# Dense S5 matrices of a two-layer trunk as 64x64 tiles in four quadrants, with the S5 input fetched in two halves

## What is computed

```python
def _s5_mixer(u, a_re, a_im, b_re, b_im, c_re, c_im, d_skip, log_dt, w_glu):
    ug = u.reshape(B, L, S5_GROUPS, S5_GROUP)           # 64 groups of 16 channels
    dt = jnp.exp(log_dt)[:, None]
    mag = jnp.exp(a_re * dt)                            # a_re, a_im: (64, 64)
    ab_re, ab_im = mag * jnp.cos(a_im * dt), mag * jnp.sin(a_im * dt)
    ...
    bb_re = cf_re * b_re - cf_im * b_im                 # (64, 64, 16)
    bb_im = cf_re * b_im + cf_im * b_re
    bu_re = jnp.einsum('blgi,gni->blgn', ug, bb_re)
    bu_im = jnp.einsum('blgi,gni->blgn', ug, bb_im)
    _, _, x_re, x_im = lax.associative_scan(...)        # x_t = ab * x_(t-1) + bu_t
    y = jnp.einsum('blgn,gin->blgi', x_re, c_re) - jnp.einsum('blgn,gin->blgi', x_im, c_im)
    y = jax.nn.gelu(y.reshape(B, L, S5_WIDTH) + d_skip * u)
    return y * jax.nn.sigmoid(y @ w_glu)
```

## Time and profile before

| | us |
|---|---|
| median of 3 runs | 1902.22 |
| lowest and highest | 1891.05, 1905.71 |
| the profiled execution | 1898.04 |
| its span (first to last instruction) | 1896.2 |
| TensorE busy in it | 1762.7 |
| VectorE, ScalarE, GpSimd busy | 961.6, 693.6, 794.6 |
| mean granted clock of TensorE | 0.963 |

### The profile page before, as it was taken

How to read it: one execution, slowest core, us unless ns; L and a number is a source line. 1 busy time by engine, 2 the same in 40 slices (tenths; PEclk the granted TensorE clock), 3 DMA queues, 4 the chain that set the end, 5 groups by cost and what they waited for, 6 DMA issues and landing times.

```text
span 1896.2 us, 28935 instructions
## 1 busy us (share of the span) xinstructions
PE 1762.7 (93%) x11959; PEld 1572.6 (83%) x11959; DVE 961.6 (51%) x1527; ACT 693.6 (37%) x1236; POOL 794.6 (42%) x492
## 2 busy tenths in 40 slices
PE   6977898999998999999997999989999799999997
PEld 5876798999887999999996987777788688888886
DVE  8997124423428985277653222533243688734223
ACT  3453332444543213233333543344456222224222
POOL 2644565433224324433343686653332332344442
PEclk8898899999999999999998999999999999999999
DMA  9455236222364573436552433542223656433432
GB/s 148 135 167 149 82 88 142 74 79 69 89 152 148 190 200 99 104 90 174 172 156 61 125 90 90 118 123 70 76 79 102 180 191 184 141 100 91 144 104 85
DMA packets 360137, 230.38 MB, mean 121 GB/s; under 512 B 49604, under 2 KB 346744, under 8 KB 357448
## 3 DMA queue, kind: packets, MB, share of 16 engines
q1 hardware_dynamic: 349480, 198.40, 39.8%
q10 hardware_dynamic: 10528, 30.15, 4.7%
HBM read 180.82 MB, written 47.15 MB: 120 GB/s over the span
## 4 chain that ended last, share of the span: by engine, by line
PE 66%; DVE 10%; DMA 7%; POOL 6%; ACT 4%; SPq 3%; issue 3%; ACTq 0%; DVEq 0%; POOLq 0%
PE ring L825 49%; DMA sb_w_raw<-in_w_in 5%; POOL sb_w_lo L667 3%; PE ring L784 3%; DVE sb_s_prod L1572 2%; DVE sb_s_mat_prod L1572 2%; PE aux L1177 2%; PE ring L806 1%; PE aux L1085 1%; SPq L570 1%; PE aux L1164 1%; PE aux L1130 1%; DVE sb_s_rot L2071 1%; PE aux L1106 1%; DVE sb_o_branch L1655 1%
## 5 line engine op out<-in xcount | busy, mean ns | idle before, releaser
L667 POOL TENSOR_TENSOR sb_w_lo<-sb_w_raw,sb_w_hi 128x1024 fp32r<-128x1024 f32 x246 | 608.7, 2476 | 1018.3 <-ACT sb_w_hi L1229 1016.2
L1229 ACT ACTIVATE sb_w_hi<-sb_w_raw 128x1024 fp32r<-128x1024 f32 x246 | 259.9, 1057 | 623.5 <-DMA sb_w_raw<-in_w_in 394.4
L825 PE MATMUL ring<-sb_u_hi,sb_w_hi 128*128 128x264 f32 (+1 forms) x2112 | 362.9, 325 | 31.5 <-DVE sb_tmp_dve L1642 21.4
L825 PEld LDWEIGHTS ring<-sb_u_hi,sb_w_hi 128*128 128x128 f32 x2112 | 308.6, 199 | 70.1 <-DVE sb_tmp_dve L1642 23.8
L825 PE MATMUL ring<-sb_u_lo,sb_w_hi 128*128 128x264 f32 (+1 forms) x2112 | 338.2, 311 | 0.0
L825 PE MATMUL ring<-sb_u_hi,sb_w_lo 128*128 128x264 f32 (+1 forms) x2112 | 334.5, 309 | 0.0
L825 PEld LDWEIGHTS ring<-sb_u_lo,sb_w_hi 128*128 128x128 f32 x2112 | 298.8, 191 | 21.2
L825 PEld LDWEIGHTS ring<-sb_u_hi,sb_w_lo 128*128 128x128 f32 x2112 | 294.2, 188 | 20.9
L1261 ACT ACTIVATE sb_tmp_act<-ring 128x528 f32<-128x528 f32 (+1 forms) x112 | 67.4, 602 | 133.0 <-PE ring L825 130.1
L825 PE MATMUL ring<-sb_y_hi,sb_w_hi 128*128 128x264 f32 (+1 forms) x504 | 88.1, 325 | 3.1 <-ACT sb_w_hi L1229 3.1
L1492 ACT ACTIVATE sb_att_scores<-sb_att_scores,sb_att_neg_max 128x208 f32<-128x208 f32 x128 | 58.4, 458 | 82.1 <-DVE sb_att_neg_max L1860 82.1
(11 more groups left out here) (328 smaller groups left out, 2585.4 us busy)
## 6 DMA issues: line engine op xcount, KB each, us to landing
sb_w_raw<-in_w_in SPq DMA_DIRECT2D x166, 512.0 KB, 4.1
sb_s_loaded<-s_matrices ACTq DMA_DIRECT2D x16, 1808.0 KB, 8.1
s_matrices<-sb_s_phase SPq DMA_DIRECT2D x16, 528.0 KB, 3.2
s_matrices<-sb_s_mbt SPq DMA_DIRECT2D x16, 512.0 KB
s_matrices<-sb_s_ca SPq DMA_DIRECT2D x16, 512.0 KB
sb_w_raw<-in_w_gla_out SPq DMA_DIRECT2D x16, 512.0 KB, 3.8
sb_w_raw<-in_w_attn_out SPq DMA_DIRECT2D x16, 512.0 KB, 3.8
sb_w_raw<-in_s_w_glu SPq DMA_DIRECT2D x16, 512.0 KB, 3.7
```

What stands on the lines that cost most here:

```text
L667: pool.tensor_tensor(WL[:, w], WR[:, w], WH[:, w].bitcast(F32), ALU.subtract).then_inc(lo_ready, 1)
L825: last = pe.matmul(RING[:, 2 * r + hf, 0:c1 - c0], w[:, n % SLOTS, kt, :], moving(b[0], xx[:, kt], c0, c1), start=(term == 0 and kt == 0), ...
L1229: act.activation(WH[:, w], WR[:, w], ACT.Copy).then_inc(hi_ready, 1)
```

## The change

The matrices `mbt`, `cam` and `toep` keep only their non-zero 64x64 parts: 64 columns for a quad in place of 128 (toep: 64 partitions' worth on the diagonal), 2336 floats per partition in place of 3616, some 1168 KB for a tile. Quads 1 and 3 have the states of their two groups in swapped halves, so that two quads together use all four quadrants. `step_inputs` has 16 logical matmuls of 64x64 in place of 8, `step_outputs` 24 in place of 12, in four groups (toep, cam, toep, cam) with three waits of TensorE for its own matmuls between them (`row_tiles_done`); the wait for the state stands behind the first toep group. Z4 is fetched in halves of four tiles, eight DMAs of 16 rows each, at ag0 and at ag3. The store to YD has 2 DMAs, the load of YZ 8 in place of 4, `load_mats` 3 in place of 1, `load_b` 8 in place of 2. `products` writes two full-partition outputs in place of four half ones. The transposes L881 become 16 matmuls of 64x64, the toep matmuls read a new buffer `mb0` with zeros in it, filled by four small copies of ScalarE at the head of `matrices_out`, for which TensorE waits (`first_power`). The skip uses a 16-column unit matrix. At the start the rows are also copied and transposed in swapped order. GpSimd zeroes `toep` and `mb0` in place of `cam`, `toep` and `mbm`.

```diff
@@ -77,7 +77,7 @@
 
-S5_FLOATS = 2 * QUADS * P + 2 * QUADS * P + QUADS * P + 2 * QUADS * STEPS
+S5_FLOATS = 2 * QUADS * 64 + 2 * QUADS * 64 + 2 * QUADS * STEPS + QUADS * 64
...
@@ -92,6 +92,7 @@
 S5_IN = 2
+Z4_PART_AT = {("ag", 0): 0, ("ag", 3): 1}
...
@@ -446,6 +451,16 @@
 
+        def load_b(queue, m):
+
+            for ri, src in enumerate((s5_b_re, s5_b_im)):
+                dst = MB[m]["b"][:, ri].rearrange("p (a x) i -> p a x i", x=2)
+                src = src[m].rearrange("(a x g) n i -> x g n a i", x=2, g=2)
+                for g in range(2):
+                    for x in range(2):
+                        rows = slice(S5_STATE * (g ^ x), S5_STATE * (g ^ x) + S5_STATE)
+                        queue.dma_start(dst[rows, :, x], src[x, g]).then_inc(s5_par, 16)
+
...
@@ -606,24 +616,33 @@
                         sp.wait_ge(z_spilled, 16 * KT * (ly + 1))
-                        for p in range(STRIDE):
-                            sp.dma_start(Z4[32 * p:32 * p + 32].rearrange("i j q c -> i (j q) c"),
-                                         ZD[ly, :, :, STRIDE - 1 - p, :].rearrange("j (q i) c -> i (j q) c", q=QUADS)
-                                         ).then_inc(steps_loaded, 16)
+                    if name in Z4_PART_AT:
+                        half = Z4_PART_AT[name]
+                        js = slice(4 * half, 4 * half + 4)
+                        for g in range(2):
+                            for p in range(STRIDE):
+                                r0 = 64 * g + 16 * p
+                                sp.dma_start(Z4[r0:r0 + 16, js].rearrange("i j q c -> i (j q) c"),
+                                             ZD[ly, js, :, STRIDE - 1 - p, :]
+                                             .rearrange("j (q g i) c -> g i (j q) c", q=QUADS, g=2)[g]
+                                             ).then_inc(steps_loaded[half], 16)
...
@@ -658,7 +677,7 @@
 
-            for name in ("cam", "toep", "mbm"):
+            for name in ("toep", "mb0"):
...
@@ -861,6 +880,9 @@
 
+            def half_rows(half):
+                return slice(64 * half, 64 * half + 64)
+
...
@@ -878,17 +900,22 @@
                     for q in range(QUADS):
-                        last = pe.transpose(AX_[:, 2 * h + ri, P * q:P * q + P],
-                                            MB[m]["mbm"][:, ri, q].rearrange("p a b -> p (a b)"), ID[:])
+                        for g in range(2):
+                            ins, outs = half_rows(g ^ (q % 2)), half_rows(g)
+                            c0 = 128 * ri + 64 * (q // 2)
+                            last = pe.matmul(AX_[outs, 2 * h + q % 2, c0:c0 + 64],
+                                             MB[m]["mbm"][ins, ri, q].rearrange("p a b -> p (a b)"), ID[ins, ins],
+                                             start=True, stop=True)
                 last.then_inc(aux_full[h], 1)
                 h = aux_take(m, ("toep", j))
-                cam, mbm = MB[m]["cam"][:, j % 2], MB[m]["mbm"]
+                cam, mb0 = MB[m]["cam"][:, j % 2], MB[m]["mb0"]
+                pe.wait_ge(first_power, 8 * m + j + 1)
                 for ri in range(2):
                     for q in range(QUADS):
-                        pe.matmul(AX_[32 * q:32 * q + 32, 2 * h, 0:P], mbm[:, ri, q, 0],
+                        pe.matmul(AX_[32 * q:32 * q + 32, 2 * h, 0:64], mb0[:, ri, q],
                                   cam[:, ri, q, 0:4].rearrange("p a b -> p (a b)"),
                                   start=(ri == 0), stop=False)
-                last = pe.matmul(AX_[:, 2 * h, 0:32], ID[:], MB[m]["dsk"][:], start=False, stop=True)
+                last = pe.matmul(AX_[:, 2 * h, 0:S5_GROUP], ID[:], MB[m]["dsk"][:], start=False, stop=True)
...
@@ -1154,30 +1184,46 @@
 
-                    if j == 0:
-                        pe.wait_ge(steps_loaded, 64 * ly + 64)
-                    pe.wait_ge(mats_in[j % 2], 16 * (4 * ly + j // 2) + 16)
+                    if j % 4 == 0:
+                        pe.wait_ge(steps_loaded[j // 4], 128 * ly + 128)
+                    pe.wait_ge(mats_in[j % 2], 48 * (4 * ly + j // 2) + 48)
                     mbt = mat_part(MSB[:, j % 2], "mbt").rearrange("p (r q m) -> p r q m", r=2, q=QUADS)
                     for ri, name in enumerate(("vre", "vim")):
                         h = aux_take(ly, (name, j))
-                        for q in range(QUADS):
-                            last = pe.matmul(AX_[:, 2 * h + q // 2, STEPS * (q % 2):STEPS * (q % 2) + STEPS],
-                                             mbt[:, ri, q, :], Z4[:, j, q, :], start=True, stop=True)
+                        for a in range(2):
+                            for x in range(2):
+                                for g in range(2):
+                                    ins, outs = half_rows(g), half_rows(g ^ x)
+                                    last = pe.matmul(AX_[outs, 2 * h + x, STEPS * a:STEPS * a + STEPS],
+                                                     mbt[ins, ri, 2 * a + x, :], Z4[ins, j, 2 * a + x, :],
+                                                     start=True, stop=True)
                         last.then_inc(aux_full[h], 1)
 
                 def step_outputs(j):
 
-                    pe.wait_ge(x_state, 8 * ly + j + 1)
                     cam = mat_part(MSB[:, j % 2], "cam").rearrange("p (r q m) -> p r q m", r=2, q=QUADS)
                     toep = mat_part(MSB[:, j % 2], "toep").rearrange("p (q m) -> p q m", q=QUADS)
                     h = aux_take(ly, ("y", j))
-                    for q in range(QUADS):
-                        dst = AX_[:, 2 * h + q // 2, STEPS * (q % 2):STEPS * (q % 2) + STEPS]
+                    for a in range(2):
+                        n = 3 * (8 * ly + j) + 2 * a + 1
+                        if a:
+                            last.then_inc(row_tiles_done, 1)
+                            pe.wait_ge(row_tiles_done, n - 1)
+                        for x in range(2):
+                            for g in range(2):
+                                rows, q = half_rows(g), 2 * a + x
+                                last = pe.matmul(AX_[rows, 2 * h + x, STEPS * a:STEPS * a + STEPS],
+                                                 toep[rows, q], Z4[rows, j, q, :], start=True, stop=False)
+                        last.then_inc(row_tiles_done, 1)
+                        pe.wait_ge(row_tiles_done, n)
+                        pe.wait_ge(x_state, 8 * ly + j + 1)
                         for ri in range(2):
-                            pe.matmul(dst, cam[:, ri, q],
-                                      XX[:, ri, q, :], start=(ri == 0), stop=False)
-                        last = pe.matmul(dst, toep[:, q], Z4[:, j, q, :],
-                                         start=False, stop=True)
+                            for x in range(2):
+                                for g in range(2):
+                                    ins, q = half_rows(g ^ x), 2 * a + x
+                                    last = pe.matmul(AX_[half_rows(g), 2 * h + x, STEPS * a:STEPS * a + STEPS],
+                                                     cam[ins, ri, q], XX[ins, ri, q, :],
+                                                     start=False, stop=(ri == 1))
...
@@ -1291,13 +1337,22 @@
 
+                act.wait_ge(mats_ready, 8 * m + j + 1)
+                for half in range(2):
+                    rows = slice(64 * half, 64 * half + 64)
+                    for x in range(2):
+                        c0 = S5_GROUP * (half ^ x)
+                        last = act.activation(MB[m]["mb0"][rows, :, x::2, c0:c0 + S5_GROUP],
+                                              MB[m]["mbm"][rows, :, x::2, 0], ACT.Copy)
+                last.then_inc(first_power, 1)
                 if j:
                     spilled(act, m, j - 1)
                 h = aux_result(act, m, ("mbt", j))
-                act.activation(MB[m]["mbt"][:].rearrange("p r q m -> p r (q m)"), aslot(h), ACT.Copy
+                act.activation(MB[m]["mbt"][:].rearrange("p r (a x) m -> p x (r a) m", x=2),
+                               aslot(h)[:, :, 0:256].rearrange("p x (b m) -> p x b m", b=4), ACT.Copy
                                ).then_inc(aux_free[h], 1)
                 h = aux_result(act, m, ("toep", j))
-                last = act.activation(MB[m]["toep"][:, 3 * 32:], AX_[:, 2 * h, 0:P], ACT.Copy)
+                last = act.activation(MB[m]["toep"][:, 48:], AX_[:, 2 * h, 0:64], ACT.Copy)
...
@@ -1329,7 +1386,11 @@
                 act.wait_ge(phase_spilled, 16 * 8 * (ly + 1))
-                act.dma_start(MSB[:, j % 2], MATD[ly, j]).then_inc(mats_in[j % 2], 16)
+                o = S5_FLOATS - QUADS * 64
+                act.dma_start(MSB[:, j % 2, 0:o], MATD[ly, j, :, 0:o]).then_inc(mats_in[j % 2], 16)
+                toep = mat_part(MATD[ly, j], "toep").rearrange("(t g i) x -> g t i x", t=STRIDE, g=2)
+                for g in range(2):
```

(39 more changed lines are left out.)

96 lines of the change are left out of this document (51 added, 45 removed).

## The result

| | before | after |
|---|---|---|
| median of 20 runs, us | 1902.98 | 1892.12 |
| lowest, highest | 1891.05, 1909.54 | 1884.84, 1900.03 |
| the profiled execution | 1898.04 | 1896.51 |
| its span; mean clock | 1896.2; 0.963 | 1894.7; 0.958 |

After to before is 0.994, 95% interval 0.9925 to 0.9956: 0.6% faster, 10.9 us. Forecast were 1872 us and a gain of some 30. The gain is about a third of the forecast, and "faster by over 1%" did not come. The time lies in the range of 1851 to 1897, but only because the range was drawn wide enough for rivals A in pairs and B (1889 and 1888); the forecast's own range ended at 1884.

What follows compares the result with a forecast made beforehand. TensorE, busy 93% of the span, was taken as the bound, with 133 us of waiting. Terms -19.6 - 5 - 5 - 10 + 11 + 1.7 = -26.9 gave 1872 us; own range 1851 to 1884, with rivals 1851 to 1897.

Steps and rivals of the forecast that it cites:

- A in pairs: S5 tiles: quadrants work only two at a time, +13 in place of -5, 1889 us; chance 0.09.
- B: S5 front: splitting the Z4 fetch moves nothing, SP's issue holds the weights; -3 for -19.6, 1888 us; chance 0.11.
- Step 1: Front of the S5 stage, both layers: halved fetch and smaller matrices land weights earlier; -19.6 us, ends -27 and -3.
- Step 2 and 3: S5 middle: later wait for the state, -5 us; steady tiles: 4.2 us against 4.57, -5 for 14 periods.
- Rival A: S5 tiles: not four quadrants at once; two at a time 1889 us, all in series 1952; chance 0.13.
- Step 4: Layer 0's matrices: VectorE saves 13 us, toep's waits for ScalarE copies mostly absorbed; net -10 us, ends -16 and +18.
- Step 5: Layer 1's matrices: VectorE's gain hidden, TensorE waits for ScalarE's copies; +11 us, ends +6 and +30.
- Rival C: Both matrix sets: waits for ScalarE replace those for VectorE, +18 and +30, 1918 us; chance 0.08.
- Step 6: Start: six S5P copies for two and two more transposes ahead of the first norm; +1.7 us, ends 0 and 3.

Runs made afterwards that it cites:

- Experiment 8: Kernel before, with Z4 fetched whole at ag0 by eight DMAs of 16 rows in place of four of 32: 1925.58 us, ratio 1.0116.
- experiment 9: Changed kernel with each half of Z4 fetched by two DMAs of 64 rows, the spill writing in read order by four DMAs a tile: 1888.92 us, ratio 0.9934.
- experiment 1: Changed kernel with ScalarE's first-power copies of layer 1's matrices moved ahead of the block's turn: 1867.21 us, ratio 0.9821 to the kernel before.
- experiment 2: Changed kernel with a tile's output matmuls reordered so that independent matmuls stand before each self-wait: 1885.26 us, ratio 0.9908.
- experiment 5: Changed kernel with both layer 1's first-power copies ahead of the block's turn and the reordered output matmuls: 1870.28 us, ratio 0.9816.
- experiment 7: Changed kernel with the first-power copies moved ahead in both layers' sets, in layer 0's ahead of log_sigmoid: 1865.33 us, ratio 0.9803.
- experiment 3: Changed kernel with all of Z4 fetched at ag0 by eight DMAs of 16 rows, not in halves: 1920.11 us, ratio 1.009.
- experiment 11: The kernel of experiment 9 with Z4 fetched whole at ag0, by two DMAs of 64 rows: 1910.83 us, ratio 1.0051.
- experiment 6: Changed kernel with the second half of Z4 fetched at mg2 1 in place of ag3: 1894.98 us, ratio 0.9955.

## Why the prediction was off, step by step

**Step 1, the front: -19.6 forecast, -11.8 measured.** The failed step is "the weights land near 564 in place of 571: 7.1 earlier, and ag6 with them, as its stop is the longest". Three things in it were wrong.

The pace: "the engines are free some 5 us sooner (half of 10.2)" halves the landing time of 32-row DMAs, but the change has DMAs of 16 rows, and those moved 132 GB/s where the others had moved 189. The weights behind the first half take 8.6 us from issue to landing (547.75 to 556.34) where they took 13.40. Experiment 8 shows it on the kernel before: 107 for 189 GB/s, 20 us slower.

The second half: it "delays ag5's or ag6's weights by up to 5 us, which three weight slots cover". ag6's weights were issued at 566 and used from 581, 15 us.

The cause of ag6's stop: in before it was not the weights of ag6. Late weights held up ag3, where VectorE's chain begins, and from there on the chain's length decided. ScalarE had ag6's weights 14 us before TensorE began ag6 at 598.65:

```profile
584.52 1.06 ACT L1229 ACTIVATE sb_w_hi<-sb_w_raw 128x1024 fp32r<-128x1024 f32 x1 [3.02 <-DMA sb_w_raw<-in_w_in]
```

What ag6 waited for was VectorE, busy 24.59 of the 25.1 us before it (experiment 9). "What is late next is VectorE's chain" stood in the text, without a length; it should have been measured. Where that chain ran in 19.27 us and the pace was 198 GB/s (experiment 9, layer 0) the front took 10.1 us less than before, about the 9.8 of the forecast; in layer 1 it was 7.4. The sign asked for, ag6's stop under 1.5 us, did not come.

**Step 2 and 3, middle and steady tiles: -10 forecast, -3.8 measured.** The parts were near: four quadrants at once, self-waits of 0.23 to 0.25 us where 0.24 was taken, 0.9 us for the Gelu's slot where 1.0 was. Outputs are 2.74 (forecast 2.5), the sum to the next block 4.26 (4.2). But the comparison was made against 4.57, a sum of rows, and this is the failed step. In the timeline of before the same stretch is 655.67 to 660.16, 4.49, and of the 0.23 that is left only a third arrives: the period from watt1 to watt2 is 16.10 us where it was 16.17. So 14 tiles give 1 us, not 5. The stops of the middle did not vanish, they moved: in after's trace there are four for a late state, 9.1 us together, where before's has two of 5.9. Two of them, at 609 and at 1569 us:

```profile
605.64 3.48 DVE L1631 TENSOR_TENSOR sb_s_state<-sb_s_prod 128x524 f32<-128x524 f32 x2
...
609.27 0.68 PE L1224 MATMUL aux<-sb_s_state,sb_s_loaded 64*64 64x132 f32 x16 [1.69 <-DVE sb_s_state L1631]
```

```profile
1568.89 0.72 PE L1224 MATMUL aux<-sb_s_state,sb_s_loaded 64*64 64x132 f32 x16 [2.21 <-DVE sb_s_state L1631]
```

The same two operations take 1.3 us at other tiles; they are long where GpSimd's L686 runs beside them. Which tiles are hit, and how many, changes from trace to trace, so that the medians of this stretch (-3.5 in layer 0, -0.3 in layer 1) say little by themselves. That GpSimd is the cause was not tested by itself.

**Rival A: wrong.** The Trainium skill's "TensorEngine Tiling (Array Packing)", Gotcha 1, was weighed for it. The trace speaks against the rule as this kernel would need it: pairs of both row halves writing one bank run at the pace of four quadrants, 16 recorded matmuls in 0.50 us. In each pair the two write different partitions of the bank; two row halves at one address were never let run together here.

**Step 4, layer 0's matrices: -10 forecast, -7.8 in the set and -5.2 behind it, up to mg0 0.** The sum looks like the 13 us that were worked out as VectorE's saving, but that is luck: the -5.2 is not VectorE's. No edit stands in that stretch, and TensorE waits the same there, 12.7 and 12.3 us. What differs is the granted clock, 0.95 before and 0.98 after (the value ahead of the last two):

```profile
194.20:359.80 165.60, 152.85 (x1206) 141.44 (x1204) 52.05 (x114) 61.67 (x117) 94.37 (x61) 0.95 0.39 98
```

```profile
189.70:350.00 160.30, 147.96 (x1206) 137.63 (x1205) 53.25 (x114) 61.26 (x116) 92.51 (x59) 0.98 0.39 102
```

Why it is higher was not tested; in experiments 1, 2 and 5 the same code takes 162.6 to 162.9 us.

In the set, the eight outputs of 820 ns became four a tile:

```profile
L1631 DVE TENSOR_TENSOR sb_s_mb<-sb_s_mat_prod 128x256 f32<-128x256 f32 x16 | 9.0, 602 | 0.3
```

TensorE's waits of 60 to 180 us, where the earlier trace rows had 27.9 for VectorE:

```profile
PE aux L915 <- ACT sb_s_mb_first L1345: 15.0, 7, 5.6
...
PE aux L906 <- DVEq L2106: 12.6, 4, 5.5
```

The sum is the same, 27.6 us. The waits for VectorE are half, as was asked for, but those for ScalarE took their place. They were not absorbed as wholly as was said: with the copies ahead (experiment 7) the set takes 145.8 us, 12.8 less than before. That is VectorE's saving as it was worked out, but TensorE's own matmuls for transposes and toep are shorter there too, 10.7 us busy for 20.4, and the two were not separated.

**Step 5, layer 1's matrices: +11 forecast, +16.0 in the stretch and -2.4 behind it.** This was the right mechanism at the wrong size, and it hid a gain. The failed step is the count for the later turns. "+2.3" for the first stop was near the 2.67 seen; "0.4" for the next was not: all five stops are 2.7 to 5.2 us, and each is followed by 0.9 to 2.3 us of lower clock, which no term had. The edge itself costs 22 to 25 us (experiment 1). "VectorE's gain is hidden" was right: before, TensorE waited for VectorE only 1.9 us there. What else the change gives came from a term that nobody wrote down, TensorE's own smaller matmuls: for transposes and toep it is busy 5.3 + 3.2 us in the stretch before, 3.5 + 2.2 in experiment 1. That and the clock (0.96, 0.99) are the 5.9 us by which experiment 1 is shorter than before.

**Rival C** named the cause and the place. Its sign came: over 28 us of waits for the first-power copies, 15.0 + 16.0 = 31.0. Its consequence, a slower kernel, did not, since in layer 0's set those waits stood largely where TensorE had waited for VectorE.

**Step 6, the start: +1.7 forecast, +2.6 measured.** The sum counted the six copies of L1673 and L1676 at 0.25 and left out the four that swap the rows (L1666, L1668). The first of those, and the copy of dt before it (1.25 us in before), ran beside GpSimd's weight splitting:

```profile
15.02 1.95 DVE L1664 COPY sb_s_dt_wide<-sb_s_dt_rows 64x128 f32<-64x128 f32 x1 [0.19 <-DVE sb_bias_rows L1660]
...
16.90 2.34 DVE L1666 COPY sb_s_rows_swapped<-sb_s_rows 128x64 f32<-128x64 f32 x1
```

In all, the terms gained less by 7.8 at the front, by 6.2 in the stage behind it and by 2.2 in layer 0's set, and cost 2.6 more at layer 1's set and 0.9 at the start; the clock behind layer 0's set gave 5.2 that no term had: -12.4 for -26.9. More than any of these differences is what stood behind step 5: a loss of 22 to 25 us that was taken as the price of the change, and was the price of where four copies stand in ScalarE's order.

## What to carry to other kernels

When an edit puts a small copy of another engine on TensorE's path, ask what stands ahead of it in that engine's order, and count for every stop the block at the lower clock that follows; here four copies of 0.2 us cost 22 to 25 us at one place of the program, and too little to be told from nothing at another. When a DMA is cut finer, take its pace from a transfer that is cut the same way, not from the bytes. Before a late transfer is priced, look whether the engine that stops had its data by then, and measure the chain that would be late next. And when a stretch came out as forecast, split it into waits, work and clock before you call the forecast right.

## What the runs showed that was not expected

- The same 528-byte packets from DRAM into SBUF move at 107 to 111 GB/s in eight DMAs of 16 partitions, at 189 in four of 32 and at 190 to 198 in two of 64, at a busy share of 1.17 to 1.26 (experiments 3, 8, 9, 11). Rows and number of DMAs were not varied apart.
- From ag3 to ag6 the same work takes VectorE 19 us with 6 us of GpSimd's weight splitting beside it, and 25 us with 11 to 13 (experiments 6, 9, 11 and before).
- Pairs of matmuls of different row halves, writing different partitions of one PSUM bank, ran beside each other, four quadrants in the time of one matmul.
- A wait of TensorE for its own last matmul costs 0.23 to 0.25 us over the pace, and next to nothing when independent matmuls stand between: a tile's outputs take 1.98 us where the groups alone are 1.90 (experiment 2).
- The same VectorE copy of 64 columns took 2.34 us beside GpSimd's tensor operation and 0.18 us alone.
